# Attention blocks of a hybrid layer: a second buffer for the transposed probabilities, the memory values in a bank of their own, values and results spread over the next block

## The chip, the cores and the metric

The kernel runs on one core of a Trainium2 chip. The metric is the device time of one execution in microseconds (us); less is better. TensorE does the matrix products, VectorE and ScalarE the elementwise work, SyncE issues the transfers. Each engine takes its instructions in the order in which they are written; engines wait for one another by semaphores that are counted up.

## The reference, cut to what matters

One encoder layer with 1024 tokens and a width of 2048: RMS norm, one input projection, three groups of heads, a gate, an output projection. The change is in the groups B and C, attention in a window and attention into 256 memory tokens:

```python
# B: 8 query heads of 64, 2 key heads; |i-j| <= 128, banded blocks of 128 queries x 384 keys
s = jnp.where(mask, einsum('bnqhgd,bnkhd->bnhgqk', qb, kw) * d ** -0.5, -inf)
m = maximum(max(s), sink);  p = exp(s - m);  p = p / (sum(p) + exp(sink - m))
o_b = einsum('bnhgqk,bnkhd->bnqhgd', p, vw) * silu(zb)
# C: 4 heads of 128 against 256 memory tokens
p = softmax(einsum('bshd,bmhd->bhsm', q, k) * d ** -0.5)
o_c = einsum('bhsm,bmhd->bshd', p, v) * silu(zc)
```

## The kernel before

Four stages run one after the other: the projections (front_stage), the delta rule of group A (delta_stage), attention (attention_stage, from about 1780 to 2023 us of the profile) and the output projection (output_stage). The first transfer of the output stage starts at 2022.95 us, after the last result of attention has been stored.

attention_stage has a preparation (keys, norms, transposed values) and then 8 blocks (BLK) of 128 queries. A block h has a slot of five units: u = 0 to 3 are pairs of window heads, u = 4 (LAST) is the memory attention with its four heads. Every engine has its own hand-written program over the same slots, and the order within an engine is the order in the code:

- VectorE, `slot`: for each u first `maxima` of the unit that comes next (row maxima and masked scores, L1418, or for the memory unit L1428), then `probabilities` of this unit (L1440 to L1453). In u = 0 the `results` of the block before come as well: `which` 0 multiplies the window values in the bank po with the gate z into out_b, `which` 1 the memory values, in the same bank po, into out_c (both L1462). In u = 1 come the `queries` of the next block (rotary, L1402 to L1409), which read the bank px.
- TensorE, `slot`: for each u first the `scores` of the unit two ahead (L1541, or L1546 for the memory unit) into one of two halves of ps, then in u = 0 the `values` of the block before, then the `transposes` of this unit's probabilities into tp (L1560, L1565), and in u = 1 `rotate` of the next block's queries into px (L1526).
- `values`: 6 products into po from pt_b (window, L1574), then 8 products into po from pt_c (memory, L1581). The second group waits until VectorE has read the first out of po.
- ScalarE: the exponentials of the next unit (`exps`, L1330 to L1337), then `take_t`, which copies the transposed probabilities from tp into pt_b (L1350) or pt_c (L1353). `take_t` of u = 0 waits until the window values of the block before have been computed, since there is one pt_b.
- SyncE: for each block `load` of the next one: its queries q (L1265, L1266) and, once both results of the block before are done, its gates z (L1269, L1270); then `store` of the block before (L1275, L1278). A load of q waits until the z load ahead of it has landed (L1264).

The PSUM memory has eight banks: ps has four, tp two, po and px one each.

Of the kernel before, what the change touches and what calls it, by code (L numbers as in the profile page):

```python
# [25 lines left out]
P = 128  # L26
# [8 lines left out]
C_HEADS = 4  # L35
# [1145 lines left out]
def attention_stage(nc, c, proj, kv_scratch, consts, mixed):  # L1181
# [9 lines left out]
    with ExitStack() as stack:  # L1191
# [15 lines left out]
        sm = n.sb("sm", [P, 2, 2, W])  # L1207
        prob = n.sb("prob", [P, 2, SEQ])
        mx, negm, rsum, diff, sinks = (n.sb(x, [P, 2, 4]) for x in ("mx", "negm", "rsum", "diff", "sinks"))
        pt_b, pt_c = n.sb("pt_b", [P, 3, 2, 4, P]), n.sb("pt_c", [P, 2, C_HEADS, P])  # L1210
        out_b, out_c = n.sb("out_b", [P, 4, P]), n.sb("out_c", [P, 4, P])
        ps = n.ps("ps", [P, 2, 2, HALF])
        tp, po, px = n.ps("tp", [P, 2, HALF]), n.ps("po", [P, HALF]), n.ps("px", [P, HALF])
# [22 lines left out]
        def after(h, k):  # L1236

            return h >= k
# [60 lines left out]
        def _(act):  # L1299
# [40 lines left out]
                                       accum_out=rsum[:, odd, i:i + 1]).then_inc(b_e, 1)  # L1340

            def take_t(h, u):
                if u == 0 and after(h, 1):
                    act.wait_ge(b_o, h * 2 - 1)
                if u == LAST and after(h, 1):
                    act.wait_ge(b_o, h * 2)
                for i in range(2):
                    act.wait_ge(b_t, h * 10 + (2 * u + i + 1))
                    if u < LAST:
                        act.activation(pt_b[:, :, i, u], tp[:, i, 0:W].rearrange("p (a n) -> p a n", n=P),  # L1350
                                       ACT.Copy).then_inc(b_td, 1)
                    else:
                        act.activation(pt_c[:, i], tp[:, i].rearrange("p (a n) -> p a n", n=P),  # L1353
                                       ACT.Copy).then_inc(b_td, 1)
# [13 lines left out]
        def _(dve):  # L1368
# [86 lines left out]
            def results(h, parity, which):  # L1455

                out, st = ((out_b, st_b), (out_c, st_c))[which]
                dve.wait_ge(b_o, h * 2 + (which + 1))
                dve.wait_ge(l_z, h * 32 + 32)
                if after(h, 1):  # L1460
                    dve.wait_ge(st, h * 16)
                dve.scalar_tensor_tensor(out[:], po[:].rearrange("p (a n) -> p a n", n=P), 0.5,  # L1462
                                         z_in[:, parity, 4 * which:4 * which + 4], ALU.mult, ALU.mult).then_inc(b_res, 1)

            def slot(h, parity, more, w):
                for u in range(U):
                    if u < LAST:
                        maxima(h, u + 1, (parity + u + 1) % 2, w)
                    elif more:
                        maxima(h + 1, 0, (parity + U) % 2, NEXT_WINDOW(h))  # L1470
                    probabilities(h, u, (parity + u) % 2)
                    if h > 0 and u == 0:
                        results(h - 1, 1 - parity, 0)
                        results(h - 1, 1 - parity, 1)
                    if more and u == 1:
                        queries(h + 1, 1 - parity)

            def NEXT_WINDOW(h):
                return 2 if h == BLK - 2 else 1
# [8 lines left out]
        def _(pe):  # L1488
# [33 lines left out]
            def rotate(h, parity):  # L1522
                pe.wait_ge(l_q, h * 32 + 32)
                if after(h, 1):
                    pe.wait_ge(b_q, h * 3)
                pe.matmul(px[:], rot_q[:], q_in[:, parity, 0:4].rearrange("p a n -> p (a n)"),  # L1526
                          start=True, stop=True).then_inc(b_rot, 1)

# [36 lines left out]
                            last = pe.transpose(tp[:, i, bass.ts(head, P)], prob[:, odd, at:at + P], c["ident"][:])  # L1565
                    last.then_inc(b_t, 1)

            def values(h, parity):
                pe.wait_ge(b_td, h * 10 + 8)
                if after(h, 1):  # L1570
                    pe.wait_ge(b_res, h * 2)
                for kc in range(3):
                    for g in range(2):
                        last = pe.matmul(po[64 * g:64 * g + 64, :], v_rows[:, h + kc, 64 * g:64 * g + 64],  # L1574
                                         pt_b[:, kc, g].rearrange("p a n -> p (a n)"), start=kc == 0, stop=kc == 2)
                last.then_inc(b_o, 1)
                pe.wait_ge(b_td, h * 10 + 10)
                pe.wait_ge(b_res, h * 2 + 1)
                for head in range(C_HEADS):
                    for m in range(2):  # L1580
                        last = pe.matmul(po[:, bass.ts(head, P)], mem_v[:, m, bass.ts(head, P)], pt_c[:, m, head],  # L1581
                                         start=m == 0, stop=m == 1)
                last.then_inc(b_o, 1)

            def slot(h, parity, more, w):
                for u in range(U):
                    if u + AHEAD < U:
                        scores(h, u + AHEAD, (parity + u) % 2, parity)
                    elif more:
                        scores(h + 1, u + AHEAD - U, (parity + u) % 2, 1 - parity)  # L1590
                    if h > 0 and u == 0:
                        values(h - 1, 1 - parity)
                    transposes(h, u, (parity + u) % 2)
                    if more and u == 1:
                        rotate(h + 1, 1 - parity)

            rotate(0, 0)
            scores(0, 0, 0, 0)
            scores(0, 1, 1, 0)
            blocks(slot)  # L1600
            values(BLK - 1, 1)


def output_stage(nc, c, mixed, w_out, x, out):
# [301 lines left out]
```

## Time and profile before

| | us |
|---|---|
| median of 3 runs | 2393.86 (2391.51 to 2399.91) |
| the profiled execution | 2397.7 |
| its span in the profile | 2395.9 |
| TensorE busy in the span | 2176.7 (91%) |
| VectorE busy | 1082.7 (45%) |
| ScalarE busy | 656.9 (27%) |
| first window values to the last result of attention | 1860.9 to 2020.2 |

The busy shares of the page are means over four stages with different limits. The attention stage has to be read by itself: by the busy time of its stretches, by who waited for whom in them, and by the order of time of one block. A block repeats every 21.65 us where TensorE's granted clock stays at 2.4 GHz. In the profile, matmuls of 32-bit data appear as two entries for each written one, and the end of a matmul is modelled, so starts are safer than ends.

### The profile page before, as it was taken

To read this page: it belongs to the slowest core of one execution; us is meant where nothing else is said; L and a number is where in the kernel's file an instruction comes from. 1 tells how busy PE (TensorE), PEld (TensorE's weight loads), DVE (VectorE), ACT (ScalarE), POOL (GpSimd) and SP (SyncE) were. 2 spreads that over 40 slices of the span, in tenths; PEclk is the share of its full clock that TensorE was granted. 3 is DMA by queue.
4 is the path that set the end of the run, shared out by engine and by line. 5 is a ranking of instruction groups with operands and counts; after the bars stand their busy time and mean duration, and the time that the engine had idled before them with its cause. 6 is when DMAs were issued, how large, how long until landed. Compare 5 with 4: busy or idle time off the path is not lost. (4 is left out here: it accounts for less than half of the span.)

```text
span 2395.9 us, 29047 instructions
## 1 busy us (share of the span) xinstructions
PE 2176.7 (91%) x11264; PEld 1806.8 (75%) x11264; DVE 1082.7 (45%) x1857; ACT 656.9 (27%) x999; POOL 313.2 (13%) x196
## 2 busy tenths in 40 slices
PE   6999999999999999999929999899967775999998
PEld 6888888888888888888818888788855443888887
DVE  7763444345335111223126676666625775422222
ACT  5511111111111101111033554444123554311111
POOL 4300000000000000000045444444200000000000
PEclk9999999999999999999969999999986988999999
DMA  6521221221122221221031111111023223633432
GB/s 225 182 99 60 79 79 53 79 79 68 64 79 79 79 78 53 79 79 62 18 125 45 63 63 41 41 63 62 10 98 90 74 59 115 254 130 134 164 134 88
DMA packets 78871, 210.92 MB, mean 88 GB/s; under 512 B 7328, under 2 KB 33056, under 8 KB 74560
## 3 DMA queue, kind: packets, MB, share of 16 engines
q1 hardware_dynamic: 69088, 174.04, 21.5%
q0 software_dynamic: 9696, 35.72, 3.8%
q8 instruction: 55, 0.90, 0.2%
q14 instruction: 32, 0.26, 0.0%
HBM read 165.11 MB, written 44.63 MB: 88 GB/s over the span
## 5 line engine op out<-in xcount | busy, mean ns | idle before, releaser
L73 PE MATMUL pr_acc<-x_hi,pr_w_lo 128*128 128x512 f32 (+1 forms) x1760 | 675.8, 384 | 25.8 <-DVE pr_w_lo L428 23.3
L74 PE MATMUL pr_acc<-x_lo,pr_w_hi 128*128 128x512 f32 (+1 forms) x1760 | 674.1, 383 | 0.0
L75 PE MATMUL pr_acc<-x_hi,pr_w_hi 128*128 128x512 f32 (+1 forms) x1760 | 674.1, 383 | 0.0
L73 PEld LDWEIGHTS pr_acc<-x_hi,pr_w_lo 128*128 128x128 f32 x1760 | 333.9, 190 | 91.3 <-issue 21.1
L74 PEld LDWEIGHTS pr_acc<-x_lo,pr_w_hi 128*128 128x128 f32 x1760 | 334.2, 190 | 63.8 <-issue 0.2
L75 PEld LDWEIGHTS pr_acc<-x_hi,pr_w_hi 128*128 128x128 f32 x1760 | 334.1, 190 | 63.8
L344 ACT ACTIVATE pr_w_hi<-pr_w_raw 128x1024 fp32r<-128x1024 f32 x118 | 124.8, 1059 | 748.5 <-PE pr_acc L75 728.8
L529 DVE TENSOR_TENSOR pr_padded<-pr_acc,pr_rstd 128x512 f32<-128x512 f32 x82 | 56.6, 692 | 518.5 <-PE pr_acc L75 518.3
L73 PE MATMUL ou_acc<-ou_w_hi,ou_m_lo 128*128 128x512 f32 x512 | 200.3, 391 | 18.7 <-DVE ou_w_lo L1701 18.7
L74 PE MATMUL ou_acc<-ou_w_lo,ou_m_hi 128*128 128x512 f32 x512 | 200.0, 391 | 0.0
L75 PE MATMUL ou_acc<-ou_w_hi,ou_m_hi 128*128 128x512 f32 x512 | 199.9, 390 | 0.0
L1701 DVE TENSOR_TENSOR ou_w_lo<-ou_w_raw,ou_w_hi 128x2048 fp32r<-128x2048 f32 x32 | 73.3, 2292 | 198.6 <-ACT ou_w_hi L1668 198.6
L252 POOL DMA_DIRECT2D proj_scratch<-pr_res x50 | 26.7, 533 | 1031.3 <-DVE pr_res L552 829.4
L428 DVE TENSOR_TENSOR pr_w_lo<-pr_w_raw,pr_w_hi 128x1024 fp32r<-128x1024 f32 x118 | 147.8, 1289 | 0.4 <-ACT pr_w_hi L344 0.4
L1668 ACT ACTIVATE ou_w_hi<-ou_w_raw 128x2048 fp32r<-128x2048 f32 x32 | 61.3, 1916 | 260.5 <-PE ou_acc L75 257.7
L73 PEld LDWEIGHTS ou_acc<-ou_w_hi,ou_m_lo 128*128 128x128 f32 x512 | 96.6, 189 | 39.2 <-ACT ou_m_hi L1673 18.9
L541 DVE SCALAR_TENSOR_TENSOR pr_conv<-pr_padded,pr_head_taps,pr_conv 128x1024 f32<-128x1024 f32 x96 | 123.3, 1285 | 3.4
L1079 PE MATMUL dl_ring<-dl_wt,dl_mt 128*128 128x128 f32 x768 | 106.1, 289 | 18.6 <-POOL dl_mt L863 14.1
L1079 PEld LDWEIGHTS dl_ring<-dl_wt,dl_mt 128*128 128x128 f32 x768 | 96.0, 197 | 29.6 <-DVE dl_wt L926 17.6
L1085 PE MATMUL dl_ring<-dl_dt,dl_wt 128*128 128x128 f32 x768 | 99.7, 285 | 17.5 <-DVE dl_wt L918 17.5
L1085 PEld LDWEIGHTS dl_ring<-dl_dt,dl_wt 128*128 128x128 f32 x768 | 95.8, 199 | 25.6 <-DVE dl_wt L918 18.9
L74 PEld LDWEIGHTS ou_acc<-ou_w_lo,ou_m_hi 128*128 128x128 f32 x512 | 96.7, 189 | 20.0
(212 smaller groups left out, 2513.4 us busy)
## 6 DMA issues: line engine op xcount, KB each, us to landing
pr_w_raw<-in_w_in SPq DMA_DIRECT2D x118, 512.0 KB, 4.7
ou_w_raw<-in_w_out SPq DMA_DIRECT2D x32, 1024.0 KB, 4.9
proj_scratch<-pr_res POOLq DMA_DIRECT2D x50, 512.0 KB, 4.7
dl_qk<-proj_scratch SPq DMA_DIRECT2D x8, 1024.0 KB, 5.0
dl_grow<-gate_rows SPq DMA_DIRECT2D x8, 1024.0 KB, 7.5
ou_x_in<-in_x SPq DMA_DIRECT2D x8, 1024.0 KB, 7.2
out<-ou_res POOLq DMA_DIRECT2D x8, 1024.0 KB, 4.7
pr_res<-in_x_t SPq DMA_DIRECT2D x11, 512.0 KB, 5.7
```

Of the source, the lines that this page charges most:

```text
L73: pe.matmul(out, w_lo, x_hi, start=first, stop=False)
L74: pe.matmul(out, w_hi, x_lo, start=False, stop=False)
L75: return pe.matmul(out, w_hi, x_hi, start=False, stop=last)
L252: pool.dma_start(proj[bass.ds(first + j, 1)].rearrange("a p n -> p (a n)"), gate_raw if kind == "g" else res[:, j % 2]).then_inc(s_st, 16)
L344: return act.activation(w_hi[:, b], w_raw[:, b], ACT.Copy).then_inc(s_hi, 1)
L428: dve.tensor_tensor(w_lo[:, b], w_raw[:, b], w_hi[:, b].bitcast(F32), ALU.subtract).then_inc(s_lo, 1)
L529: dve.tensor_tensor(body[:, bass.ts(h, HALF)], acc[:, bank + h], rstd[:, bass.ts(h, HALF)], ALU.mult).then_inc(s_taken, 1)
L541: dve.scalar_tensor_tensor(conv[:], src, w, conv[:], ALU.mult, ALU.add).then_inc(s_tap, 1)
L1079: last = pe.matmul(ring[:, b, bass.ts(i, P)], mt[:, 2 * b + i], d[:, 2 * b + i], start=True, stop=True)
L1085: last = pe.matmul(as_blocks(ring[:, b, bass.ts(i, P)], LEVELS[level]), zz[:, 2 * b + i], left_d(parity, 2 * b + i, 1, level), start=True, ...
L1668: act.activation(w_hi[:, q % 2], w_raw[:, q % 2], ACT.Copy).then_inc(w_h, 1)
L1701: dve.tensor_tensor(w_lo[:, q % 2], w_raw[:, q % 2], w_hi[:, q % 2].bitcast(F32), ALU.subtract).then_inc(w_l, 1)
```

## The change

The transposed window probabilities get a second buffer (`pt_b[:, h % 2]`), and ScalarE's `take_t` of u = 0 waits for the window values of two blocks ago in place of one. `values` is split in two. `window_values` stays in u = 0 of the next block, but comes behind that unit's transposes. `memory_values` moves to the end of u = 2, writes px instead of po, and no longer waits for VectorE's first result; it waits for the rotary product to be read out of px (b_q). `rotate` waits in turn until the memory result is read out of px. On VectorE the first result moves from u = 0 to u = 1, the second to u = 3. SyncE's code is the same.

```diff
@@ attention_stage, buffers
-        pt_b, pt_c = n.sb("pt_b", [P, 3, 2, 4, P]), n.sb("pt_c", [P, 2, C_HEADS, P])
+        pt_b, pt_c = n.sb("pt_b", [P, 2, 3, 2, 4, P]), n.sb("pt_c", [P, 2, C_HEADS, P])
@@ ScalarE, take_t
-                if u == 0 and after(h, 1):
-                    act.wait_ge(b_o, h * 2 - 1)
+                if u == 0 and after(h, 2):
+                    act.wait_ge(b_o, h * 2 - 3)
...
-                        act.activation(pt_b[:, :, i, u], tp[:, i, 0:W].rearrange("p (a n) -> p a n", n=P),
+                        act.activation(pt_b[:, h % 2, :, i, u], tp[:, i, 0:W].rearrange("p (a n) -> p a n", n=P),
@@ VectorE, results and slot
-                dve.scalar_tensor_tensor(out[:], po[:].rearrange("p (a n) -> p a n", n=P), 0.5,
+                dve.scalar_tensor_tensor(out[:], (po, px)[which][:].rearrange("p (a n) -> p a n", n=P), 0.5,
...
-                    if h > 0 and u == 0:
+                    if h > 0 and u == 1:
                         results(h - 1, 1 - parity, 0)
-                        results(h - 1, 1 - parity, 1)
                     if more and u == 1:
                         queries(h + 1, 1 - parity)
+                    if h > 0 and u == 3:
+                        results(h - 1, 1 - parity, 1)
@@ TensorE, rotate
+                if after(h, 3):
+                    pe.wait_ge(b_res, h * 2 - 4)
@@ TensorE, values
-            def values(h, parity):
+            def window_values(h):
                 pe.wait_ge(b_td, h * 10 + 8)
                 if after(h, 1):
-                    pe.wait_ge(b_res, h * 2)
+                    pe.wait_ge(b_res, h * 2 - 1)
...
-                                         pt_b[:, kc, g].rearrange("p a n -> p (a n)"), start=kc == 0, stop=kc == 2)
+                                         pt_b[:, h % 2, kc, g].rearrange("p a n -> p (a n)"), start=kc == 0, stop=kc == 2)
                 last.then_inc(b_o, 1)
+
+            def memory_values(h):
                 pe.wait_ge(b_td, h * 10 + 10)
-                pe.wait_ge(b_res, h * 2 + 1)
+                pe.wait_ge(b_q, min(h * 3 + 8, 3 * BLK))
...
-                        last = pe.matmul(po[:, bass.ts(head, P)], mem_v[:, m, bass.ts(head, P)], pt_c[:, m, head],
+                        last = pe.matmul(px[:, bass.ts(head, P)], mem_v[:, m, bass.ts(head, P)], pt_c[:, m, head],
@@ TensorE, slot
+                    transposes(h, u, (parity + u) % 2)
                     if h > 0 and u == 0:
-                        values(h - 1, 1 - parity)
-                    transposes(h, u, (parity + u) % 2)
+                        window_values(h - 1)
                     if more and u == 1:
                         rotate(h + 1, 1 - parity)
+                    if h > 0 and u == 2:
+                        memory_values(h - 1)
```

TensorE in one block before, from the scores that open it (c_ident is the identity matrix of a transpose, kvt holds the memory keys):

```order
L1541 MATMUL at_ps<-at_k_pad,at_q_rope 128x384 x2
L1574 MATMUL at_po<-at_pt_b,at_v_rows 64x512 x6
L1581 MATMUL at_po<-at_pt_c,at_mem_v 128x128 x8
L1560 MATMUL at_tp<-c_ident,at_prob 128x128 x6
L1541 MATMUL at_ps<-at_k_pad,at_q_rope 128x384 x2
L1560 MATMUL at_tp<-c_ident,at_prob 128x128 x6
L1526 MATMUL at_px<-at_q_in,at_rot_q 128x512
L1546 MATMUL at_ps<-at_kvt,at_q_mem 128x256 x4
L1560 MATMUL at_tp<-c_ident,at_prob 128x128 x6
L1541 MATMUL at_ps<-at_k_pad,at_q_rope 128x384 x2
```

The same part of TensorE's program now (the lines of the changed kernel are 3 to 5 further on):

```order
L1544 MATMUL at_ps<-at_k_pad,at_q_rope 128x384 x2
L1563 MATMUL at_tp<-c_ident,at_prob 128x128 x6
L1577 MATMUL at_po<-at_pt_b,at_v_rows 64x512 x6
L1544 MATMUL at_ps<-at_k_pad,at_q_rope 128x384 x2
L1563 MATMUL at_tp<-c_ident,at_prob 128x128 x6
L1529 MATMUL at_px<-at_q_in,at_rot_q 128x512
L1549 MATMUL at_ps<-at_kvt,at_q_mem 128x256 x4
L1563 MATMUL at_tp<-c_ident,at_prob 128x128 x6
L1586 MATMUL at_px<-at_pt_c,at_mem_v 128x128 x8
L1544 MATMUL at_ps<-at_k_pad,at_q_rope 128x384 x2
```

The window values have moved behind the first transposes, and the memory values from there to behind the third, into px.

VectorE at the turn from u = 0 to u = 1, before (the multiply L1446 ends the probabilities of u = 0, the first L1418 begins the maxima of u = 2):

```order
L1442 RECIPROCAL at_rsum<-at_rsum 128x2
L1446 TENSOR_SCALAR at_prob<-at_prob,at_rsum 128x384 x2
L1462 SCALAR_TENSOR_TENSOR at_out_b<-at_po,at_z_in 128x512
L1462 SCALAR_TENSOR_TENSOR at_out_c<-at_po,at_z_in 128x512
L1418 ISA at_sm,at_mx<-at_ps,at_window,at_rq 128x384
```

And now, one unit later, and further on at the end of u = 3:

```order
L1442 RECIPROCAL at_rsum<-at_rsum 128x2
L1446 TENSOR_SCALAR at_prob<-at_prob,at_rsum 128x384 x2
L1462 SCALAR_TENSOR_TENSOR at_out_b<-at_po,at_z_in 128x512
L1402 TENSOR_TENSOR at_q_rope<-at_q_in,at_qcos 128x512
L1404 TENSOR_SCALAR at_q_mem<-at_q_in,at_cw 128x512
...
L1442 RECIPROCAL at_rsum<-at_rsum 128x2
L1446 TENSOR_SCALAR at_prob<-at_prob,at_rsum 128x384 x2
L1462 SCALAR_TENSOR_TENSOR at_out_c<-at_px,at_z_in 128x512
L1418 ISA at_sm,at_mx<-at_ps,at_window,at_rq 128x384
```

The two results no longer follow each other: the maxima and probabilities of u = 1 now stand ahead of the first, the queries and two further units between the two.

## Rows read from the trace of the kernel before

**Rows 1.** The page: busy us of each engine, share of span, instructions.

```profile
PE 2176.7 (91%) x11264; PEld 1806.8 (75%) x11264; DVE 1082.7 (45%) x1857; ACT 656.9 (27%) x999; POOL 313.2 (13%) x196
```

**Rows 2.** Busy time by stretch, one steady block, with its columns.

```profile
core 0: us, PE busy (x) PEld busy (x) DVE busy (x) ACT busy (x) POOL busy (x), PEclk, DMA share, GB/s
...
1883.00:1905.10 22.10, 15.61 (x90) 9.10 (x88) 16.19 (x55) 12.43 (x41) 0.00 (x0) 1.00 0.25 73
```

**Rows 3.** Waits, 1860 to 2016 us: total us, times, longest.

```profile
DVE at_out_b L1462 <- PE at_po L1574: 17.4, 7, 3.2
...
DVE at_out_c L1462 <- PE at_po L1581: 15.4, 7, 2.2
...
DVE at_q_tmp L1406 <- PE at_px L1526: 3.0, 6, 0.5
...
DVE at_sm L1418 <- PE at_ps L1541: 0.6, 2, 0.3
```

**Rows 4.** Order of time, VectorE and TensorE: start, us, engine, line, operation.

```profile
1882.58 2.79 PE L1574 MATMUL at_po<-at_pt_b,at_v_rows 128*64 128x512 f32 x12
...
1885.43 0.69 DVE L1462 SCALAR_TENSOR_TENSOR at_out_b<-at_po,at_z_in 128x512 f32<-128x512 f32 x1 [2.24 <-PE at_po L1574]
...
1886.26 2.02 PE L1581 MATMUL at_po<-at_pt_c,at_mem_v 128*128 128x128 f32 x16 [0.89 <-DVE at_out_b L1462]
...
1888.32 0.69 DVE L1462 SCALAR_TENSOR_TENSOR at_out_c<-at_po,at_z_in 128x512 f32<-128x512 f32 x1 [2.21 <-PE at_po L1581]
...
1888.87 0.92 PE L1541 MATMUL at_ps<-at_k_pad,at_q_rope 64*128 64x384 f32 x4
...
1888.93 0.61 DVE L1418 CUSTOM_DVE_ANT_0 at_sm<-at_ps,at_window,at_rq 128x384 f32<-128x384 f32 x1
...
1890.39 0.16 DVE L1440 TENSOR_TENSOR at_rsum<-at_rsum,at_sinks 128x2 f32<-128x2 f32 x1
...
1891.27 0.88 PE L1560 MATMUL at_tp<-c_ident,at_prob 128*128 128x128 f32 x6 [1.48 <-DVE at_prob L1446]
...
1891.45 0.68 DVE L1402 TENSOR_TENSOR at_q_rope<-at_q_in,at_qcos 128x512 f32<-128x512 f32 x1
...
1891.98 1.02 PE L1526 MATMUL at_px<-at_q_in,at_rot_q 128*128 128x512 f32 x2
...
1893.04 0.69 DVE L1406 TENSOR_TENSOR at_q_tmp<-at_px,at_sin 128x512 f32<-128x512 f32 x1 [0.51 <-PE at_px L1526]
...
1894.38 0.61 DVE L1418 CUSTOM_DVE_ANT_0 at_sm<-at_ps,at_window,at_rq 128x384 f32<-128x384 f32 x1
...
1896.72 0.88 PE L1560 MATMUL at_tp<-c_ident,at_prob 128*128 128x128 f32 x6 [1.98 <-DVE at_prob L1446]
...
1903.70 0.16 DVE L1440 TENSOR_TENSOR at_rsum<-at_rsum,at_sinks 128x2 f32<-128x2 f32 x1
...
1904.24 2.79 PE L1574 MATMUL at_po<-at_pt_b,at_v_rows 128*64 128x512 f32 x12
```

**Rows 5.** Order of time of SyncE's queue, and landing of query loads.

```profile
1889.04 0.37 SPq L1269 DMA_DIRECT2D at_z_in<-proj_scratch  x1
...
1893.69 0.38 SPq L1265 DMA_DIRECT2D at_q_in<-proj_scratch  x1
...
DMA to landing us min/median/max: 3.0/3.4/3.9
```

**Rows 6.** A low-clock stretch: busy time, and order of time.

```profile
1920.00:1924.00 4.00, 3.15 (x12) 1.65 (x10) 3.78 (x16) 3.77 (x13) 0.00 (x0) 0.50 0.00 0
...
1920.98 1.54 PE L1560 MATMUL at_tp<-c_ident,at_prob 128*128 128x128 f32 x6 [0.80 <-DVE at_prob L1446]
```

**Rows 7.** Order of time, end of the attention stage.

```profile
2008.75 0.18 DVE L1449 RECIPROCAL at_rsum<-at_rsum 128x4 f32<-128x4 f32 x1 [1.30 <-ACT at_prob L1337]
...
2012.06 4.47 PE L1574 MATMUL at_po<-at_pt_b,at_v_rows 128*64 128x512 f32 x12
...
2019.48 0.69 DVE L1462 SCALAR_TENSOR_TENSOR at_out_c<-at_po,at_z_in 128x512 f32<-128x512 f32 x1 [2.21 <-PE at_po L1581]
```

More of the change, by code:

```diff
@@ L1600, in _ @@
             blocks(slot)
-            values(BLK - 1, 1)
+            window_values(BLK - 1)
+            memory_values(BLK - 1)
 def output_stage(nc, c, mixed, w_out, x, out):
```

## The prediction

> **What bounds the kernel now.** I read the page first: TensorE is busy 91% of the span [rows 1]. That is a mean over four stages and says nothing of the attention stage, which alone is changed. So I read the busy time of its stretches next: in one steady block of 22.1 us, without any low clock, TensorE is busy 15.6, VectorE 16.2 and ScalarE 12.4 us [rows 2]. No engine is full; something makes them wait in turn. The waits of that stage name it: VectorE waited 17.4 us over 7 blocks for the window values (L1574) and 15.4 for the memory values (L1581), and little for anything else: 3.0 us for the rotary product [rows 3]. The order of time of one block shows the rest. The reader is to see there that VectorE's instructions follow one another without a gap except at three places: 2.24 us ahead of out_b, 2.21 ahead of out_c, 0.51 ahead of L1406 [rows 4]. So **VectorE's queue sets the block's period**, 1904.24 - 1882.58 = 21.66 us [rows 4], and 2.24 + 2.21 + 0.51 = 4.96 us of it are waits. TensorE's own waits ahead of transposes (1.48, 1.98 us) are for VectorE and cost nothing by themselves. Without a wait VectorE would need 21.66 - 4.96 = 16.70 us.
>
> **The change, part by part.** I call T the start of a block's first probabilities on VectorE, L1440 (1903.70 in the rows, just ahead of the values at 1904.24) [rows 4].
>
> *What is removed.* Both waits in u = 0, 4.45 us a block. ScalarE's wait for the old window values goes too, but ScalarE is not the late one.
>
> *The first result, in u = 1.* TensorE now does the transposes of u = 0 first. They can start once the first of two multiplies is done: 0.88 us after L1440 (1891.27 - 1890.39), and the next operation follows 0.71 later (1891.98 - 1891.27) [rows 4]. The window values thus start at T + 1.59, and VectorE could use them 2.85 later (1885.43 - 1882.58) [rows 4], at T + 4.44. Meanwhile VectorE does the probabilities of u = 0 (1.06, from 1890.39 to 1891.45), the maxima of u = 2 (1.46, from 1888.93 to 1890.39) and the probabilities of u = 1 (1.06): it arrives at T + 3.58 [rows 4]. **A wait of 0.86 us stays.**
>
> *The rotary product.* Behind the window values (2.79) stand scores (0.92), transposes 0.71 and the rotation with its 1.06 until VectorE can read (1893.04 - 1891.98) [rows 4]. It is readable at T + 1.59 + 2.79 + 0.92 + 0.71 + 1.06 = T + 7.07, or 0.3 earlier since ends are modelled. VectorE has the first result (0.61, from 1888.32 to 1888.93) at T + 5.05, and then 1.08 of query work that needs no product (1893.04 - 1891.45 - 0.51): T + 6.13 [rows 4]. Wait: 0.6 to 0.9, I take 0.7. It takes the place of the 0.51.
>
> *The memory values, in u = 2.* Now behind the third transposes. VectorE ends the queries 1.34 later (1894.38 - 1893.04), at T + 8.17, does maxima (1.46) and as far as the first multiply (0.88): transposes at T + 10.5, memory values at 11.2, readable 2.06 later (1888.32 - 1886.26) [rows 4], at T + 13.3. VectorE arrives there after two more probabilities and the memory maxima: 8.17 + 1.46 + 1.06 + about 1.5 + 1.06 = T + 13.25. Wait 0 to 0.1. Its wait for px to be read is covered: L1406 is over 4 us before. The new wait of the rotation for the second result is covered by most of a block.
>
> *New block.* 16.70 + 0.86 + 0.7 + 0.05 = 18.3 us, **3.35 less**. It applies to the six blocks with queries: 20.1 us. TensorE needs at most its 15.6 [rows 2], ScalarE 12.4, so neither is the bound.
>
> *The last block* has no queries. Before, it waited 2.2 + 2.2 at the results and 1.30 at L1449 for the exponentials [rows 3, 7] = 5.7. After: 0.86, and at L1449 the second result (0.61) now fills part of the 1.30: 0.7. Gain 5.7 - 1.55 = 4.15 us.
>
> *The tail.* After the last transposes the memory values now follow the window values without waiting 0.84 for out_b (as 1886.26 - 1885.43 in rows 4), and the end of the first need not be awaited: 1.0 us. Nothing hides this: the output stage starts behind the last store.
>
> *Low clock.* Between 1860 and 2016 us TensorE's granted clock fell three times to 0.50, that is from 2.4 to 1.2 GHz, for 3.5 to 7 us [one of them in rows 6], each time just after it had sat idle 2 us ahead of the third transposes (L1560, 1.98 us in rows 4), and once more at the end. Six transposes then take 1.54 us [rows 6] instead of 0.88. Before, this work lay mostly beside VectorE's: the window values' wait was 17.4 - 7 x 2.24 = 1.7 longer, the maxima's 0.6 [rows 3, 4]: 2.3 us for all three. After the change the 2 us idle stays where it is (T + 8.5 to T + 10.5: the queries and the maxima still stand ahead), but the memory values and the next scores stand right behind it, and VectorE is just in time for them. A low stretch of 3.5 us there doubles at most 1.8 us of work: 1.8 us lost; one of 7 us up to 3.5. I take three at 1.8 = 5.4, so 3.1 more than before.
>
> The Trainium skill (TensorE: Matmul & The Clock Gate, "A second HAM failure mode: psum-queue depth-cycling") tells of a kernel whose short TensorE pauses between groups of matmuls made the clock swing between its two levels. By it, fewer pauses mean fewer swings, and the 3.1 us would turn into a gain; the rows here speak of the one long pause, which the change leaves.
>
> *Sum.* 20.1 + 4.15 + 1.0 - 3.1 = 22.2 us. The profiled execution goes from 2397.7 to 2375.5; against the median of 2393.86 that is **2371.7 us**.
>
> **The rivals.**
>
> *The query load becomes the bound.* The z load waits for the second result, which moves from u = 0 to u = 3; the stores and the next query load are queued behind it on SyncE. From the result's end (1889.01) the z load goes out at 1889.04, and the query load not before 1893.69, when z has landed [rows 5]: 4.7 us, and 0.43 + 3.4 to 3.9 until the queries' second half has landed [rows 5], in all 8.5 to 9.0. The second result ends at T + 13.9, so the queries are there at T + 22.4 to 22.9, and the next block wants them at T + 18.3 + 5.05 = T + 23.35. Cover: 0.45 to 0.95 us. If the same transfers in shorter blocks take 1.5 us longer, the loop is (13.9 - 5.05) + 10.5 = 19.4, 1.1 us a block over five blocks: 2377. For it: the cover is thin. Against it: the burst itself has the same transfers in the same order as now.
>
> *The low clock costs more:* in each of six blocks a long stretch at 3.5 us, 21 instead of 2.3: 25.25 - 18.7 = 6.5 us gained, 2387. For it: the idle of 2 us stands in every block. Against it: before, three of six blocks had none in spite of it.
>
> *No low clock,* the tail's included: 25.25 + 2.3 + 2.6 (1.7 from the values at 2012.06, 4.47 instead of 2.79 [rows 4, 7], 0.9 from the transposes ahead) = 30.1: 2364.
>
> *Slower:* TensorE stays at 1.2 GHz through most of the blocks. It then needs twice its 14 to 15.6 us, 28 to 31 a block, against 21.66 now: seven blocks at +6.5 and up give 2439. It decides from about a third of the blocks' time at the low level ((21.66 - 18.3) / (28 - 18.3)); before, it was some 17 of 155 us. Against it: TensorE will be busier per us than before.
>
> **How the numbers follow.** Forecast 0.60; query load 0.13; costlier low clock 0.13; no low clock 0.10; TensorE low throughout 0.04. The likeliest gives 2371.7. The range goes from 2360 (no low clock, with the 4 us by which runs differ) to 2382, which holds the query load with a landing still longer; it leaves out the dear low clock and the slow case, 0.17. A change of under 0.3% (7.2 us) can't be told from none. Faster by more: 0.60 + 0.13 + 0.10 and half of the dear clock, 0.90; within: the other half and a little of the last, 0.07; slower 0.03.
>
> **What would show it.** The period between window values 18.3 us where the clock is full; VectorE's wait ahead of out_b 0.86, ahead of L1406 0.7, ahead of out_c under 0.2; no idle of ScalarE ahead of the first copy to pt_b beyond 1 us; the query load issued 4 to 5 us behind the second result and no wait for it on VectorE or TensorE. A wait of L1402 or of the rotation for a transfer would make the first rival right; waits for px over 1 us or a period over 19 at full clock would show that I have mis-sized TensorE's queue in u = 1.

## The result, and the profile after

| us | before | after |
|---|---|---|
| median of 5 runs | 2397.34 (2391.51 to 2399.91) | 2376.53 (2372.66 to 2379.48) |
| profiled execution | 2397.7 | 2377.5 |
| its span | 2395.9 | 2375.7 |

The ratio is 0.9912, with a 95% interval of 0.9899 to 0.9925: 20.8 us faster. The forecast was 22.2 us less, 2371.7 us with a range of 2360 to 2382. Of the 4.8 us between the forecast and the median, 3.5 are the start: with more runs the median of before is 2397.3, not 2393.9.

The busy time of the engines on the page is as good as unchanged against [rows 1]; only the span is shorter:

```profile
PE 2175.2 (92%) x11264; PEld 1810.1 (76%) x11264; DVE 1083.4 (46%) x1857; ACT 657.5 (28%) x999; POOL 312.2 (13%) x196
```

The waits of the attention stage, 1860 to 2000 us (total us, times, longest), against [rows 3]:

```profile
DVE at_out_b L1462 <- PE at_po L1577: 9.8, 8, 3.9
...
DVE at_out_c L1462 <- PE at_px L1586: 7.6, 6, 1.5
...
DVE at_q_tmp L1406 <- PE at_px L1529: 4.9, 6, 0.8
...
DVE at_sm L1418 <- PE at_ps L1544: 1.7, 6, 0.6
...
DVE at_rsum L1449 <- ACT at_prob L1337: 0.7, 1, 0.7
```

The wait for the window values has fallen from 17.4 us in 7 blocks to 9.8 in 8, of which 3.9 are the last at the stage's end; the wait for the memory values (now in px) from 15.4 to 7.6, and those 7.6 are not in all blocks: five with a low clock have about 1.3 us each, and the stage's end has 1.28.

VectorE in a block with full clock, in order of time (start, us, engine, line, operation, idle before), against [rows 4]:

```profile
1881.48 0.16 DVE L1440 TENSOR_TENSOR at_rsum<-at_rsum,at_sinks 128x2 f32<-128x2 f32 x1
...
1886.00 0.69 DVE L1462 SCALAR_TENSOR_TENSOR at_out_b<-at_po,at_z_in 128x512 f32<-128x512 f32 x1 [0.84 <-PE at_po L1577]
...
1888.50 0.69 DVE L1406 TENSOR_TENSOR at_q_tmp<-at_px,at_sin 128x512 f32<-128x512 f32 x1 [0.81 <-PE at_px L1529]
...
1894.96 0.69 DVE L1462 SCALAR_TENSOR_TENSOR at_out_c<-at_px,at_z_in 128x512 f32<-128x512 f32 x1
...
1899.94 0.16 DVE L1440 TENSOR_TENSOR at_rsum<-at_rsum,at_sinks 128x2 f32<-128x2 f32 x1
```

And TensorE in the same block:

```profile
1882.35 0.88 PE L1563 MATMUL at_tp<-c_ident,at_prob 128*128 128x128 f32 x6 [0.26 <-DVE at_prob L1446]
...
1883.16 2.79 PE L1577 MATMUL at_po<-at_pt_b,at_v_rows 128*64 128x512 f32 x12
...
1887.44 1.02 PE L1529 MATMUL at_px<-at_q_in,at_rot_q 128*128 128x512 f32 x2
...
1892.18 0.88 PE L1563 MATMUL at_tp<-c_ident,at_prob 128*128 128x128 f32 x6 [1.99 <-DVE at_prob L1446]
...
1892.89 1.95 PE L1586 MATMUL at_px<-at_pt_c,at_mem_v 128*128 128x128 f32 x16
```

The reader is to see T = 1881.48, the window values at T + 1.68, out_b at T + 4.52 after a wait of 0.84, the rotary product read at T + 7.02 after 0.81, the third transposes at T + 10.70 after 1.99 of idle, and out_c at T + 13.48 with no wait at all. The next block's L1440 is at 1899.94: a period of 18.46 us.

But this block is the only one of its kind among the six. The window values (L1577) start at 1863.10, 1883.16, 1901.62, 1921.72, 1941.81, 1961.86 and 1981.91: periods of 20.06, **18.46**, 20.10, 20.09, 20.05 and 20.05. In the third of them:

```profile
1910.64 1.52 PE L1563 MATMUL at_tp<-c_ident,at_prob 128*128 128x128 f32 x6 [1.99 <-DVE at_prob L1446]
...
1911.95 2.99 PE L1586 MATMUL at_px<-at_pt_c,at_mem_v 128*128 128x128 f32 x16
...
1914.98 0.69 DVE L1462 SCALAR_TENSOR_TENSOR at_out_c<-at_px,at_z_in 128x512 f32<-128x512 f32 x1 [1.46 <-PE at_px L1586]
...
1915.83 0.62 DVE L1418 CUSTOM_DVE_ANT_0 at_sm<-at_ps,at_window,at_rq 128x384 f32<-128x384 f32 x1 [0.16 <-PE at_ps L1544]
```

The memory values take 2.99 us in place of 1.95, out_c waits 1.46 us for them and the next maxima 0.16 more: 1.6 us. The busy time by stretch (columns as in [rows 2]) of the clean block and of the one behind it shows what differs; the granted clock falls from 1.00 to 0.92:

```profile
1883.16:1901.62 18.46, 14.94 (x88) 8.97 (x87) 16.02 (x55) 12.06 (x40) 0.00 (x0) 1.00 0.28 81
...
1901.62:1921.72 20.10, 16.58 (x88) 10.63 (x87) 16.11 (x55) 12.23 (x40) 0.00 (x0) 0.92 0.28 81
```

Looked at more closely, it is 0.50, half the speed, while the memory values run:

```profile
1912.00:1913.00 1.00, 1.00 (x6) 1.00 (x6) 0.86 (x6) 0.85 (x3) 0.00 (x0) 0.50 0.00 0
```

In all five such blocks it stays so for about 3.5 us, and begins close to the start of the third transposes, which follow the idle of 2 us, or at most 1.1 us behind it.

### The profile page after: what moved, and what is told of

It is laid out like the page before. It is cut to its first block and busy times, and to the rows that moved or that the text cites. A ratio compares the mean times of both kernels' runs of the same rounds, so it can differ in the third digit from the quotient of the medians.

```text
span 2375.7 us, 29046 instructions
## 1 busy us (share of the span) xinstructions
PE 2175.2 (92%) x11264; PEld 1810.1 (76%) x11264; DVE 1083.4 (46%) x1857; ACT 657.5 (28%) x999; POOL 312.2 (13%) x196
## 5 line engine op out<-in xcount | busy, mean ns | idle before, releaser
L1085 PEld LDWEIGHTS dl_ring<-dl_dt,dl_wt 128*128 128x128 f32 x768 | 95.8, 199 | 25.6 <-DVE dl_wt L918 18.9
L75 PEld LDWEIGHTS ou_acc<-ou_w_hi,ou_m_hi 128*128 128x128 f32 x512 | 96.8, 189 | 20.4
```

Of the source, the lines that this page charges most:

```text
L75: return pe.matmul(out, w_hi, x_hi, start=False, stop=last)
L1085: last = pe.matmul(as_blocks(ring[:, b, bass.ts(i, P)], LEVELS[level]), zz[:, 2 * b + i], left_d(parity, 2 * b + i, 1, level), start=True, ...
```

## The experiments

Each was run beside the kernel before, on the same chip with it; the changed kernel itself was not run again beside them. So kernels of different sets are compared by their ratios to before, whose intervals of about 0.0017 each way (4 us) are wider than most of the steps below. The steps are therefore read from the traces, one execution of each kernel. A "low stretch" is a time in which the granted clock is 0.50. "Period" is from one start of the window values to the next, from the profile; before, the six were four at 21.65 and two at 22.97 and 22.84, though three of them held a low stretch: the first of these cost nothing.

### The second buffer alone

```diff
-        pt_b, pt_c = n.sb("pt_b", [P, 3, 2, 4, P]), n.sb("pt_c", [P, 2, C_HEADS, P])
+        pt_b, pt_c = n.sb("pt_b", [P, 2, 3, 2, 4, P]), n.sb("pt_c", [P, 2, C_HEADS, P])
...
-                if u == 0 and after(h, 1):
-                    act.wait_ge(b_o, h * 2 - 1)
+                if u == 0 and after(h, 2):
+                    act.wait_ge(b_o, h * 2 - 3)
```

The copy and the window values index the buffer by `h % 2`.

> The kernel before with one part of the change alone: two buffers for the transposed window probabilities, so that ScalarE's first copy of a block no longer waits for the window values of the block before. All else is as before. My theory: ScalarE is not late, VectorE's two waits at the results stay at 2.24 and 2.21 us, the block stays at 21.65 us and the ratio to before at 1.000 (within 0.2%). Rival (the buffer is what frees the block): ScalarE's idle of 4.9 us ahead of the first copy goes and the block shortens by more than 0.5 us, ratio 0.998 or less.

Measured: ratio 1.0003 (0.9993 to 1.0014). Periods 21.65 to 21.67 and one of 23.00. VectorE waits in seven blocks as before:

```profile
DVE at_out_b L1462 <- PE at_po L1574: 16.6, 7, 3.2
...
DVE at_out_c L1462 <- PE at_po L1581: 15.4, 7, 2.2
```

ScalarE's idle ahead of its first copy even stays (34.6 us in 7 blocks, now put down to the transposes): in the old order the first transposes are behind the values anyway. The buffer alone does nothing. That the first wait adds up to 16.6 us and not to 17.4 is the low clock: only one low stretch cost time here, against two before.

### The memory values' own bank alone

```diff
-                pe.wait_ge(b_res, h * 2 + 1)
+                pe.wait_ge(b_q, min(h * 3 + 5, 3 * BLK))
...
-                        last = pe.matmul(po[:, bass.ts(head, P)], ...
+                        last = pe.matmul(px[:, bass.ts(head, P)], ...
```

VectorE's second result reads px, and the rotation waits until it has been read.

> The kernel before with another part alone: the memory values go into px directly behind the window values in u = 0, without waiting for VectorE's first result; both results stay in u = 0. My theory: the wait ahead of out_b stays 2.24, the one ahead of out_c falls from 2.21 to about 1.2 (2.56 + 2.06 of TensorE against 2.85 + 0.61), so 1.05 us a block over seven blocks and 0.9 at the end: 8 us, ratio 0.9965. Rival (TensorE's waits for the bank cost nothing, only the place of the results counts): ratio 1.000, since VectorE waits as long.

Measured: 0.9958 (0.9941 to 0.9974), periods 20.74 and one of 22.01, so 0.91 us a block, a little less than the 1.05 expected.

```profile
DVE at_out_b L1462 <- PE at_po L1576: 16.6, 7, 3.1
...
DVE at_out_c L1462 <- PE at_px L1583: 9.0, 7, 1.3
```

The wait for the memory values fell from 2.21 to 1.28 us each, the other stayed. This is what the bank is worth where both results stay together: TensorE no longer stands still for 0.89 us.

### The changed kernel with one bank

```diff
-                pe.wait_ge(b_q, min(h * 3 + 8, 3 * BLK))
+                pe.wait_ge(b_res, h * 2 + 1)
...
-                        last = pe.matmul(px[:, bass.ts(head, P)], ...
+                        last = pe.matmul(po[:, bass.ts(head, P)], ...
```

VectorE's second result reads po, the rotation no longer waits for a result, and the window values wait for the second result of the block before in place of the first.

> The changed kernel, but the memory values stay in po: they wait for the first result, which VectorE has taken out some 5 us before, and the window values of the next block wait for the second result. My theory (the spreading alone makes the gain, the bank of their own nothing): period of a block 18.5 us at full clock and 20.1 with a low stretch as in the changed kernel, ratio 0.991; only the end of the stage loses 0.8 us, as the last memory values wait for the last out_b. Rival (the bank is needed): blocks 1 us longer or more, ratio 0.994 or above.

Measured: 0.9925 (0.9908 to 0.9942), with periods of 18.47, 20.05, 18.46, 20.10, 20.10 and 20.05: the same two values as in the changed kernel. Only the last memory values wait:

```profile
1993.70 2.02 PE L1584 MATMUL at_po<-at_pt_c,at_mem_v 128*128 128x128 f32 x16 [0.89 <-DVE at_out_b L1462]
```

Once the values are spread, the bank is worth nothing in the blocks. The ratio alone could not have said so: its interval reaches from under the theory's 0.991 to over the rival's 0.994.

### The changed kernel with one buffer

```diff
-                if u == 0 and after(h, 2):
-                    act.wait_ge(b_o, h * 2 - 3)
+                if u == 0 and after(h, 1):
+                    act.wait_ge(b_o, h * 2 - 1)
```

There is one pt_b, without the index `h % 2`.

> The changed kernel with one buffer for the transposed window probabilities: ScalarE's first copy waits until the window values of the block before are computed, which stand behind the same unit's transposes. My theory: the copy then starts at T + 4.4 in place of T + 1.7 us, the exponentials queued behind it end at T + 6.7, and VectorE wants them at T + 9.6: nothing lost, ratio 0.991. Rival (the second buffer is needed now that the values are late): the exponentials or the second transposes are late and the block grows by 0.5 us or more, ratio 0.9925 or above.

Measured: 0.9927 (0.9910 to 0.9944), periods of 18.47, 18.47, 20.09, 20.05, 20.06 and 18.46. ScalarE does wait for the window values:

```profile
1886.43 0.87 ACT L1350 ACTIVATE at_pt_b<-at_tp 128x384 f32<-128x384 f32 x2 [2.73 <-PE at_po L1577]
...
1891.86 0.61 ACT L1330 ACTIVATE at_prob<-at_sm,at_negm 128x384 f32<-128x384 f32 x1 [2.51 <-DVE at_diff L1426]
```

and is idle again for 2.5 us ahead of the next exponentials, because VectorE is not ready: the wait is covered. The ratio by itself lies on the rival's side (0.9925 or above), but its interval holds the theory's 0.991 too, and no block is longer than in the changed kernel, which is what the rival needed. So in the blocks the spread order keeps its gain without the bank and without the buffer, and neither makes it alone. That the spreading needs neither of them when both are left out together is likely from this, but was not run.

### The memory values first

What remains is the 1.6 us of five blocks of the changed kernel. TensorE's idle of 2 us is ahead of the third transposes; the memory values would fit into it.

```diff
+                    if h > 0 and u == 2:
+                        memory_values(h - 1)
                     transposes(h, u, (parity + u) % 2)
...
-                    if h > 0 and u == 2:
-                        memory_values(h - 1)
```

> The changed kernel with TensorE's memory values moved ahead of the third transposes, into its idle of 2 us. My theory (that idle brings on the low clock, and the memory values behind it make it dear: five blocks at 20.05 against 18.46 us): no low stretch, every block 18.4 us, 8 us less than the changed kernel, ratio to before 0.9880. Rival (low stretches come whatever TensorE does there): they stay, but nothing late stands behind them; up to 1.2 us a block comes back and the granted clock of the stage stays under 0.95, ratio 0.989 to 0.991.

Measured: 0.9905 (0.9890 to 0.9920), which cannot be told from the changed kernel. The theory (no low stretch) missed; the rival had the ratio, but its stretches were to stay as they were. The periods are 18.28 four times, and 19.53 and 19.75. Two blocks still have a low stretch, in another place, for instance over the last transposes and the scores behind them:

```profile
1896.22 0.92 PE L1544 MATMUL at_ps<-at_k_pad,at_q_rope 64*128 64x384 f32 x4 [0.71 <-ACT at_prob L1337]
...
1898.29 1.55 PE L1568 MATMUL at_tp<-c_ident,at_prob 128*128 128x128 f32 x8 [1.15 <-DVE at_prob L1453]
...
1899.76 1.65 PE L1544 MATMUL at_ps<-at_k_pad,at_q_rope 64*128 64x384 f32 x4
...
1901.46 0.62 DVE L1418 CUSTOM_DVE_ANT_0 at_sm<-at_ps,at_window,at_rq 128x384 f32<-128x384 f32 x1 [0.71 <-PE at_ps L1544]
```

The six blocks together are 6.4 us shorter (112.4 against 118.8). 1.2 are lost in the last block, where TensorE now does the memory values ahead of transposes that nothing delays (13.84 against 12.65), and 1.7 in the tail, which had a low stretch here and none in the changed kernel. What remains of the move is 3.5 us. So there are low stretches without an idle of 2 us. Both start beside the last transposes, which follow an idle of 1.15 and of 1.34 us (1.15 in these rows).

### The memory values twice

```diff
+                    if h > 0 and u == 2:
+                        memory_values(h - 1, False)
                     transposes(h, u, (parity + u) % 2)
...
                     if h > 0 and u == 2:
                         memory_values(h - 1)
```

With `False` the products are the same, but no semaphore is counted up.

> The changed kernel with the memory values computed twice: once in TensorE's idle ahead of the third transposes, with nobody told, and again at their place behind them, with the same result. TensorE has 1.9 us more to do a block, and VectorE waits for the same late copy. My theory (the idle brings on the low clock): no low stretch in the blocks, each 18.5 us, ratio 0.988 as with the move, though TensorE does more. Rival (the gain of a move comes from the earlier result, not from the clock): blocks of 20.05 us or longer stay, ratio 0.991 or above.

Measured: 0.9888 (0.9871 to 0.9906), six periods of 18.46 or 18.48. Busy time by stretch, first the changed kernel, then this one; the second number behind the window is TensorE's busy time, the last but two its granted clock. Up to 1980 us each further stretch of 20 us reads 0.91 in the one and 1.00 in the other:

```profile
1880.00:1900.00 20.00, 16.33 (x96) 10.14 (x98) 17.50 (x62) 12.97 (x43) 0.00 (x0) 1.00 0.35 101
...
1900.00:1920.00 20.00, 16.48 (x88) 10.60 (x86) 16.01 (x55) 12.13 (x39) 0.00 (x0) 0.91 0.26 78
```

```profile
1880.00:1900.00 20.00, 17.36 (x108) 11.56 (x109) 17.55 (x61) 13.08 (x43) 0.00 (x0) 1.00 0.36 107
...
1900.00:1920.00 20.00, 18.03 (x111) 11.45 (x109) 17.42 (x62) 13.48 (x41) 0.00 (x0) 1.00 0.33 95
```

TensorE does 1.9 us more work in each block, VectorE takes the same result equally late, and the six blocks are 8.0 us shorter (110.8 against 118.8). In the last block 1.2 us are lost, as with the memory values first. The low stretches were the whole difference between 18.46 and 20.05, since the order in which VectorE gets its data is the same. That filling the pause takes them away is borne out by all traces together: with the new order and the pause of 2 us left (the changed kernel, one bank, one buffer, and the late query load below) 17 of 24 blocks had a low stretch; with the memory values in the pause (this kernel, the one before and the three that follow with this order) 4 of 30. Whether here the place of the added work counts or its amount was not separated: the same 1.9 us put elsewhere were not tried. Nor does the pause decide alone, for the old order with the same pause (before, the buffer, the bank) had 7 of 18. The Trainium skill (TensorE: Matmul & The Clock Gate, "A second HAM failure mode: psum-queue depth-cycling") describes short pauses between groups of matmuls that make the clock swing and cost throughput; this pair of traces agrees, with a granted clock of 0.91 and 1.00 and 8.0 us between them.

### The rotation early

With the memory values first, the rotation directly behind the window values:

```diff
-                    if more and u == 1:
+                    if more and u == 0:
                         rotate(h + 1, 1 - parity)
```

> The kernel with the memory values first, and the rotation moved up to directly behind the window values, ahead of the next scores and transposes. My theory: VectorE's wait of 0.81 us ahead of L1406 goes, six blocks of 17.65 us, 4.9 us less than with the memory values first alone, ratio 0.986. Rival (the query load, issued about 4 us behind the second result, is late for the earlier rotation): TensorE waits for the transfer behind the window values and the block stays above 18 us.

Measured: 0.9873 (0.9856 to 0.9889). Periods 17.38 three times, 17.56, 18.62 and 18.63. No wait for the rotary product is left in the waits of the blocks (VectorE, 1860 to 1982 us), only these for TensorE's values and scores:

```profile
DVE at_out_b L1462 <- PE at_po L1577: 6.6, 7, 1.5
...
DVE at_sm L1418 <- PE at_ps L1544: 1.8, 3, 1.1
```

At full clock it gained 0.9 us a block, a little more than the wait, and the query load was in time. The expectation had 17.65 for all six, counted from 18.46; two blocks of 18.6 hold a low stretch. The waits also show 0.8 us of TensorE's weight load for the query load, three times; the next section says why that is no wait of this kind.

### The first result between the query products

This kernel keeps the memory values first and the early rotation.

```diff
                 dve.tensor_scalar(q_mem[:, parity], q_in[:, parity, 4:8], cw_[:, 0:1], None, ALU.mult).then_inc(b_mem, 1)
+                if between:
+                    results(h - 2, parity, 0)
                 dve.wait_ge(b_rot, h + 1)
```

> The kernel before this one in the list, and VectorE's first result moved behind the two query products that need no rotation. My theory: its wait of 0.84 us for the window values goes as well, blocks of 16.8 us, which is VectorE's work alone, another 5 us less, ratio 0.984. Rival (the query load becomes the bound): the queries are wanted at T + 20.4 us, counted from the block before, and land at T + 20.0 to 20.9: waits of L1402 or of the rotation for the transfer of 0.3 us or more a block, and a ratio of 0.985 or above.

Measured: 0.9856 (0.9839 to 0.9873). Periods 16.88, 16.88, 16.89, 17.01, 16.89, 16.89, with full clock in all six:

```profile
1880.00:1900.00 20.00, 18.11 (x100) 9.81 (x96) 18.74 (x62) 13.42 (x44) 0.00 (x0) 1.00 0.29 85
...
1900.00:1920.00 20.00, 18.10 (x104) 11.39 (x105) 18.93 (x64) 12.92 (x41) 0.00 (x0) 1.00 0.27 79
```

VectorE is busy 18.7 to 18.9 of 20 us, so it sets the pace by its work. The ratio of 0.9856 lies on the rival's side of 0.985, with an interval that holds both; the blocks are as the theory has them (16.8). Did the query load become the bound? The waits name it four times, ahead of TensorE's weight load, for instance here:

```profile
1913.03 2.80 PE L1579 MATMUL at_po<-at_pt_b,at_v_rows 128*64 128x512 f32 x12
...
1915.04 0.69 DVE L1402 TENSOR_TENSOR at_q_rope<-at_q_in,at_qcos 128x512 f32<-128x512 f32 x1
...
1915.75 0.30 PEld L1531 LDWEIGHTS at_px<-at_q_in,at_rot_q 128*128 128x128 f32 x2 [0.81 <-DMA at_q_in<-proj_scratch]
1915.75 1.13 PE L1531 MATMUL at_px<-at_q_in,at_rot_q 128*128 128x512 f32 x2
...
1916.92 0.69 DVE L1408 TENSOR_TENSOR at_q_tmp<-at_px,at_sin 128x512 f32<-128x512 f32 x1 [0.19 <-PE at_px L1531]
```

That is no delay by the load. The same 0.81 us stand ahead of the rotation's weight load in all six blocks, also in the first two, where the profile puts them down to nothing ("issue"), and the rotation's product starts 2.72 or 2.73 us behind the window values each time, without a wait of its own. VectorE shows how near the load is: the queries' second half, issued at 1911.55, landed 3.5 us later, at 1915.05, just as L1402 began. Against the first two blocks L1402 starts up to 0.23 us later, and the wait ahead of L1408 behind it is shorter by as much (0.30 down to 0). So the cover of the load is used up here, but nothing is lost yet. The block of 17.01 us is long for another reason, 0.23 us between two short VectorE instructions (L1442 and L1444) of its memory unit.

### The last block put right

The kernel of the last section, with this:

```diff
-                    if h > 0 and u == 2:
+                    if h > 0 and u == 2 and more:
                         memory_values(h - 1)
                     transposes(h, u, (parity + u) % 2)
+                    if u == 2 and not more:
+                        memory_values(h - 1)
```

> The kernel with the first result between the query products, and in the last block the memory values behind the third transposes again, since there are no queries there whose time they could fill. Theory: six blocks of 16.9 us as before, the last 12.7 in place of 14.7 us, 1.2 us of it from the order and the rest if no low stretch falls there; ratio to before 0.985. Rival (the last block is long for another reason): 14 us or more remain.

Measured: 2360.53 us, 0.9852 (0.9833 to 0.9872), the same six periods and the last 12.64:

```profile
1964.02 2.79 PE L1579 MATMUL at_po<-at_pt_b,at_v_rows 128*64 128x512 f32 x12
...
1970.77 1.95 PE L1588 MATMUL at_px<-at_pt_c,at_mem_v 128*128 128x128 f32 x16
...
1976.66 4.49 PE L1579 MATMUL at_po<-at_pt_b,at_v_rows 128*64 128x512 f32 x12
```

The block came out as expected, 12.64 in place of 14.72 us. Of this 2.1 us the whole stage, up to the first transfer of the output stage, got 1.0: the low stretch at the end now lies over the last window values, which take 4.49 us against 3.44 without the edit and 2.8 at full clock. In the whole time 1.0 us cannot be told (0.9852 against 0.9856). **This version beats both kernels**: it is 36 us below before, and by the ratios some 14 us below the changed one.

### The query load later

The changed kernel, with this:

```diff
+                if after(h, 3):
+                    sp.wait_ge(st_c, h * 16 - 32)
                 sp.dma_start(q_in[:, parity, 0:4], proj_block(T_BQ, h)).then_inc(l_q, 16)
```

> The changed kernel, but the load of the queries also waits until the store of the second result has landed, which is 1.4 us later than the z load's landing (1877.19 + 0.5 + 3.7 against 1899.51 in the clean block). My rival of the prediction says that the cover of this load is 0.45 to 0.95 us: then VectorE waits 0.5 to 0.9 us for the transfer ahead of L1402 in the blocks without a low stretch, about 19.2 us instead of 18.46, and less or nothing in the blocks of 20.05 us. If the cover is over 1.4 us, nothing changes: blocks of 18.46 and 20.05 us and a ratio of 0.991.

(The time 1877.19 in it is a slip for 1897.19.) Measured: 0.9917 (0.9897 to 0.9937). Of the five loads one was late, after a landing of 4.8 us:

```profile
1903.39 0.38 SPq L1267 DMA_DIRECT2D at_q_in<-proj_scratch  x1
...
1908.68 0.69 DVE L1404 TENSOR_TENSOR at_q_rope<-at_q_in,at_qcos 128x512 f32<-128x512 f32 x1 [1.19 <-DMA at_q_in<-proj_scratch]
```

That block took 20.65 us, the other low ones 20.05 to 20.09. Every load of this execution went out in a block with a low stretch, so the case that the expectation names did not come up. The cover of the unchanged load is read better from the changed kernel: in its clean block the second result's z load goes out at 1895.67 and the query load 3.84 us later,

```profile
1895.67 0.37 SPq L1269 DMA_DIRECT2D at_z_in<-proj_scratch  x1
...
1899.51 0.38 SPq L1265 DMA_DIRECT2D at_q_in<-proj_scratch  x1
```

its second half 0.42 later with a landing of 3.5, so at 1903.4, while VectorE's L1402 begins at 1905.07: 1.6 us of cover, not 0.45 to 0.95. The late load of the experiment fits: with the median landing of 3.3 a low block of the changed kernel has 2.2 us of cover (1884.4 against 1886.61), and 1.6 us more delay and 1.5 more landing gave about 0.9 us of wait, 1.19 measured. It is the only block of all these traces that the query load made longer.

## Why the prediction was right, and where it was off

From the first L1440 of the block with results to the first transfer of the output stage, the profile went from 162.57 to 141.42 us, 21.1 less. (The whole profiled execution became 20.2 shorter: that first L1440 came 1.0 us later than before, and for that no cause was sought.) By the steps:

| term | forecast | measured |
|---|---|---|
| wait left ahead of out_b | 0.86 | 0.84 |
| wait ahead of L1406 | 0.7 | 0.81 |
| wait ahead of out_c, full clock | 0 to 0.1 | 0 |
| block, full clock | 18.3 | 18.46 |
| low clock in the six blocks | 3 x 1.8 = 5.4 | 5 x 1.6 = 8.0 |
| the same before | 2.3 | 0 + 1.3 + 1.2 = 2.5 |
| gain of six blocks | 17.0 | 13.6 |
| gain of the last block, to its last transposes | 4.15 | 4.0 |
| gain of the tail | 1.0 | 3.5 |

**What bounds the block** was read rightly: VectorE's queue, with two waits at its results. The removed waits went, the waits that took their place had the size that the sum gave them, within 0.11 us, and their places in the block were right within 0.2. The bank alone, the buffer alone and the changed kernel without one or the other show that these parts were rightly costed at nothing in the blocks; the bank's 0.9 us exists only in the old order, where the results stand together.

**The first term that was off is the low clock.** Its mechanism was right: the pause of 2 us stays, the memory values stand right behind it, VectorE is just in time for them, and 1.6 us a stretch is near the 1.8 taken. The number of stretches was not. I carried three over from before, and in the profiled execution it was five, so the low clock took 5.5 us more than before and not 3.1. Nothing in the rows gave a number; the kernels with one bank and with one buffer, whose blocks are otherwise the same, had four and three of six. Three to five may as well differ from one execution to the next: only one of each kernel was profiled, and the five runs of the changed kernel lie 6.8 us apart, as much as four stretches cost. The passage of the Trainium skill that the prediction names (TensorE: Matmul & The Clock Gate, "A second HAM failure mode: psum-queue depth-cycling") led me to say that fewer pauses mean fewer swings; I did not put that into the sum, and the trace goes the other way: TensorE is busy 14.94 of 18.46 us in the clean block, before 15.6 of 22.1 [rows 2], and had five low stretches against three. The long pause, which the change had left, is what they follow. The rival of a clock that is low throughout stayed far off: about 17 of the 119 us of the six blocks were low, and it decides from a third.

**The second is the tail,** which balanced the first. Before, a low stretch lay over the last transposes and the window values (4.47 us in [rows 7]); after, none did:

```profile
1993.54 1.09 PE L1568 MATMUL at_tp<-c_ident,at_prob 128*128 128x128 f32 x8 [2.11 <-DVE at_prob L1453]
...
1994.56 2.80 PE L1577 MATMUL at_po<-at_pt_b,at_v_rows 128*64 128x512 f32 x12
...
1997.28 2.05 PE L1586 MATMUL at_px<-at_pt_c,at_mem_v 128*128 128x128 f32 x16
...
1999.37 0.69 DVE L1462 SCALAR_TENSOR_TENSOR at_out_c<-at_px,at_z_in 128x512 f32<-128x512 f32 x1 [1.28 <-PE at_px L1586]
...
2002.84 0.83 SPq L1640 DMA_DIRECT2D ou_res<-mixed_scratch  x2
```

The transposes took 1.02 instead of 1.90 and the window values 2.84 instead of 4.52 until read, 2.55 us together; without them the tail gained 0.94, against 1.0 forecast. I had named this sum as part of the case without low clock and kept it out of the likeliest one. So the total of 21.1 against 22.2 is so near by luck in part: -2.4 from the low clock in the blocks, -1.0 from the period below and -0.15 from the last block stand against +2.5 from the tail, where a low stretch was missing in this execution (with one bank it was missing too, with one buffer it was there, 4.49 us for the window values).

**The period at full clock** is 0.16 over the forecast: 0.11 from the rotary product and 0.11 from VectorE's own work, 16.81 instead of 16.70 (18.46 - 0.84 - 0.81), less some 0.07 in the two other waits.

**The query load** was a rival with too thin a cover: I took the longest time from the result to the query load in the rows (4.7 us) and a landing of up to 3.9; in the changed kernel it was 3.8 to 3.9, just under the 4 to 5 that I gave as a sign, and the landing 3.5 in the clean block. Its mechanism is real, as the delayed load with its wait of 1.19 us shows, but in the blocks of 18.46 us 1.6 us are still left, and even at 16.9 us, where the cover is gone, it costs nothing.

## What to carry to other kernels

Where an engine in strict order waits twice in a row for a pair of results, spread the results over the next block's work before adding buffers or banks: with either of these left out the blocks kept the whole gain. Then look at the pause that the spreading leaves on TensorE: work that is not urgent belongs into the pause, not behind it, for behind it the work ran at half the clock just when somebody waited for it. A change of order that is right in the steady block has to be looked at again in the last one, where the work that covered it is missing. And before a wait is believed, look for it in a block where its cause is absent: the 0.81 us that the profile put down to a transfer stood there too.

## What the runs showed of the hardware

Adding 1.9 us of matmuls to each block made six blocks 8.0 us shorter, since the granted clock stayed at 1.00. The number of low stretches in otherwise equal blocks differed from kernel to kernel by no rule that these runs show (three to five of six in the changed kernel, with one bank and with one buffer, one execution each), while their price there was the same to 0.05 us each time, 20.05 to 20.10 against 18.46. With the new order and an idle of 2.0 us ahead of the third transposes 17 of 24 blocks had a low stretch; with that idle filled 4 of 30, two of them beside idles of only 1.15 and 1.34 us. What decides between a block with one and a block without was not tried.
